# Expert rows of both tables gathered as one, into a ring of 15 places, in a two-block transformer kernel

## The reference

```
qh = (x @ w_q).reshape(tokens, 8 heads, 2, 128);  scores = qh . sub_keys       # 2 x 128 scores a head
s_top, i_top = top_k(scores, 16);  cand = s_top[0] + s_top[1]                  # 16 x 16 sums
c_s, c_pos = top_k(cand, 16);  e_idx = number of the expert at c_pos           # 16 of 16384 experts
g = softmax(c_s);  u = expert_u[e_idx];  v = expert_v[e_idx]                   # rows of 1024 floats
a = gelu(x . u);   out = sum over 8 heads and 16 experts of (g * a) * v
```

## Time and profile before

| | |
|---|---|
| median of 3 runs | 2082.24 us (2077.01 to 2084.2) |
| profiled execution | span 2089.8 us from first to last instruction; its time outside the span is not recorded |
| busy, of the span | TensorE 1440.7, VectorE 1273.9, ScalarE 670.7, GpSimd 716.9 us |
| moved by DMA | 466.82 MB, of which 271.61 MB in the queue that holds the gathers |

### The profile page before, as it was taken

One profiled execution on the slowest core, in us unless ns is written; L12 is line 12 of the kernel. 1 busy time (PEld: TensorE's weight loads), 2 busy tenths in 40 slices (PEclk: granted clock), 3 DMA queues, 4 the chain that ended last, 5 costly groups with the idle time before them and its releaser, 6 DMA issues.

```text
span 2089.8 us, 23542 instructions
## 1 busy us (share of the span) xinstructions
PE 1440.7 (69%) x8468; PEld 1178.3 (56%) x8468; DVE 1273.9 (61%) x2141; ACT 670.7 (32%) x963; POOL 716.9 (34%) x629
## 2 busy tenths in 40 slices
PE   3999999998999999998999824443333233322345
PEld 3889989997889989997889822221111011101111
DVE  2655665554645665555445787676767676777763
ACT  2544635444544544444554411101111101111101
POOL 1010000000110000004000177677777777776775
PEclk8999999999999999999999967777677666767679
DMA  9644454655543455654545489898988888888897
GB/s 169 203 141 135 141 182 152 192 187 158 181 142 122 150 173 162 195 189 138 168 138 162 139 295 330 302 313 307 319 309 318 282 301 294 310 311 303 309 354 259
DMA packets 236976, 466.82 MB, mean 223 GB/s; under 512 B 15960, under 2 KB 136968, under 8 KB 236856
## 3 DMA queue, kind: packets, MB, share of 16 engines
q0 software_dynamic: 74432, 271.61, 37.7%
q1 hardware_dynamic: 162424, 193.65, 28.9%
HBM read 461.02 MB, written 4.19 MB: 223 GB/s over the span
## 4 chain that ended last, share of the span: by engine, by line
PE 45%; issue 14%; DMA 13%; DVE 12%; POOL 11%; ACT 4%; SPq 0%; DVEq 0%; POOLq 0%; ACTq 0%
POOL arena L1994 11%; PE acc L537 9%; PE acc L539 9%; PE acc L538 9%; DMA arena<-in_peer_v,arena 9%; PE att L537 3%; DMA arena<-in_w_in 3%; PE att L539 3%; PE att L538 3%; DVE w_lo L532 2%; ACT w_hi L526 2%; PE acc L1495 2%; PE acc L1496 1%; DVE arena L1846 1%; PE att L640 1%
## 5 line engine op out<-in xcount | busy, mean ns | idle before, releaser
L532 DVE TENSOR_TENSOR w_lo<-arena,w_hi 128x2048 fp32r<-128x2048 f32 x176 | 404.6, 2300 | 330.6 <-ACT w_hi L526 327.9
L1495 PE MATMUL acc<-arena,gate_raw 128*128 128x512 f32 x256 | 166.1, 735 | 543.6 <-DMA arena<-in_peer_v,arena 515.2
L1495 PEld LDWEIGHTS acc<-arena,gate_raw 128*128 128x128 f32 x256 | 46.2, 218 | 650.0 <-DMA arena<-in_peer_v,arena 570.6
L526 ACT CAST w_hi<-arena 128x2048 fp32r<-128x2048 f32 x176 | 334.8, 1905 | 211.8 <-DMA arena<-in_w_in 71.9
L1994 POOL DMA_INDIRECT arena<-in_peer_u,arena x256 | 340.0, 1328 | 167.9 <-issue 73.1
L1846 DVE SCALAR_TENSOR_TENSOR arena<-arena 128x1024 f32<-128x1024 f32 x256 | 302.2, 1221 | 62.1 <-DMA arena<-in_peer_u,arena 60.8
L1994 POOL DMA_INDIRECT arena<-in_peer_v,arena x256 | 304.7, 1190 | 84.5 <-issue 71.7
L1859 DVE SCALAR_TENSOR_TENSOR x_res<-arena,x_res 128x1024 f32<-128x1024 f32 x128 | 164.5, 1285 | 197.4 <-DMA arena<-in_peer_v,arena 195.9
L537 PE MATMUL acc<-xa_hi,w_hi 128*128 128x256 f32 x928 | 269.8, 291 | 20.3 <-DVE w_lo L532 17.6
L538 PE MATMUL acc<-xa_hi,w_lo 128*128 128x256 f32 x928 | 265.1, 286 | 0.0
L539 PE MATMUL acc<-xa_lo,w_hi 128*128 128x256 f32 x928 | 265.0, 286 | 0.0
(11 more groups left out here) (259 smaller groups left out, 2695.5 us busy)
## 6 DMA issues: line engine op xcount, KB each, us to landing
arena<-in_w_in SPq DMA_DIRECT2D x72, 1024.0 KB
arena<-in_w_up SPq DMA_DIRECT2D x32, 1024.0 KB
arena<-in_w_down SPq DMA_DIRECT2D x32, 1024.0 KB
arena<-in_w_branch_m SPq DMA_DIRECT2D x8, 1024.0 KB
arena<-in_w_branch_a SPq DMA_DIRECT2D x8, 1024.0 KB
arena<-in_w_out SPq DMA_DIRECT2D x8, 1024.0 KB
arena<-in_peer_w_q SPq DMA_DIRECT2D x8, 1024.0 KB
arena<-toep SPq DMA_DIRECT2D x2, 2048.0 KB, 11.7
```

The lines of the kernel that those rows point to most:

```text
L526: nc.scalar.copy(w_hi[:, s, :], raw[r]).then_inc(S["hi_ready"], mark("hi_ready", ("u2" if second else "u", u)))
L532: nc.vector.tensor_tensor(w_lo[:, s, :], raw[u % RAW_RING], w_hi[:, s, :].bitcast(F32), ALU.subtract).then_inc(S["lo_ready"], mark("lo_rea ...
L1495: nc.tensor.matmul(sums[0][:], diag[j // 2 % 2], rows_ring[j][:, 0:512], start=first, stop=last)
```

## The change

The two tables are laid side by side outside the timed kernel, so that row e holds the `u` row and then the `v` row of expert e: 8 KB. One gather brings both. There are 256 "items" n (256 gathers of 1.049 MB). `rows_ring` has 15 places of 8 KB a partition. Five (`EARLY`) are free when the attention part is over; the other ten (`LATE`) lie over `xb_hi`, `xb_lo`, the `w_hi` and `w_lo` rings and the `raw` buffers, and are free when the last unit `pq` 7 is done. The first ten items use the five early places only.

VectorE now does only dots (`row_dot`). TensorE does all sums over `v` halves, in groups of four items, with four `diag` buffers; Gelu and the coefficients go by fours too. `route` is cut in four parts, which stand between the dots.

```diff
+GROUP_ROWS = 4
+EARLY, LATE, EARLY_ITEMS = 5, 10, 10
+def ring_places():
+    return [n % EARLY if n < EARLY_ITEMS else (n - EARLY_ITEMS + EARLY) % (EARLY + LATE) for n in range(ITEMS)]
...
-        rows_ring = [area("bias", i * D, D) for i in range(4)] + [area("mo", i * D, D) for i in range(2)]
-        rows_ring += [area("mv", 0, D), area("ak", 1296, D)]
+        rows_ring = [area("bias", 0, ROW), area("bias", ROW, ROW), area("mo", 0, ROW), row_over("xa_hi", 0), row_over("xa_lo", 0)]
+        rows_ring += [row_over("xb_hi", 0), row_over("xb_lo", 0)] + [row_over("w_hi", i) for i in range(RING)]
+        rows_ring += [row_over("w_lo", i) for i in range(RING)] + raw
-        diag = [gate_flat[:, i * P:(i + 1) * P] for i in range(2)]
+        diag = [gate_flat[:, i * P:(i + 1) * P] for i in range(4)]
...
+            def rows_times_coefficients(q):
+                t = q * GROUP_ROWS // SLOTS
...
+                for n in range(q * GROUP_ROWS, (q + 1) * GROUP_ROWS):
+                    first, last = n % SLOTS == 0, n % SLOTS == SLOTS - 1
+                    pe.wait_ge(S["diag_ready"], n + 1)
+                    nc.tensor.matmul(row_sums[t][0][:], diag[n % 4], rows_ring[PLACE[n]][:, D:D + 512], start=first, stop=last)
+                    nc.tensor.matmul(row_sums[t][1][:], diag[n % 4], rows_ring[PLACE[n]][:, D + 512:ROW], start=first,
+                                     stop=last).then_inc(S["rows_multiplied"], 1)
...
-                    odd_rows(i - 2)
+                    if i in (5, 6):
+                        rows_times_coefficients(i - 5)
...
+            def group_diagonals(q):
+                n0 = q * GROUP_ROWS
+                if n0 % P_TOP == 0:
+                    weight_exp(n0 // P_TOP)
+                d = dots[:, n0:n0 + GROUP_ROWS]
+                act.wait_ge(S["rows_used"], n0 + GROUP_ROWS)
+                nc.scalar.activation(d, d, ACT.Gelu).then_inc(S["gelu_ready"], mark("gelu_ready", q))
+                act.wait_ge(S["coef"], at("coef", q))
+                for n in range(n0, n0 + GROUP_ROWS):
+                    if n >= 4:
+                        act.wait_ge(S["rows_multiplied"], n - 4 + 1)
+                    nc.scalar.activation(diag[n % 4], ident[:], ACT.Copy, scale=dots[:, n:n + 1]).then_inc(S["diag_ready"], 1)
...
+            def row_dot(n):
+                row = rows_ring[PLACE[n]][:, 0:D]
+                dve.wait_ge(S[f"gathered{PLACE[n]}"], 16 * (USES_BEFORE[n] + 1))
+                nc.vector.scalar_tensor_tensor(row, row, 1.0, hn[:, n // SLOTS, :], ALU.mult, ALU.mult,
+                                               accum_out=dots[:, n:n + 1]).then_inc(S["rows_used"], 1)
...
-                    experts(i - 1, later)
+                    if later:
+                        split_lo(dve, later, True)
+                    if i == 2:
+                        dve.wait_ge(S["xn_ready"], at("xn_ready", TT - 1))
+                        for part in range(4):
+                            route(1, part)
+                    elif i == 3:
+                        for n in range(0, 4):
+                            row_dot(n)
+                    elif i == 4:
+                        row_dot(4)
+                        coefficients(0)
+                        for n in range(5, 8):
+                            row_dot(n)
+            for part in range(2):
+                route(2, part)
+            for n in range(8, ITEMS):
+                row_dot(n)
+                if n % GROUP_ROWS == 0:
+                    coefficients(n // GROUP_ROWS - 1)
+                g, k = n // P_TOP, n % P_TOP
+                if g + 2 < ALL_HEADS and k % 4 == 2:
+                    route(g + 2, k // 4)
...
+            for n in range(ITEMS):
+                if n % P_TOP == 0:
+                    g = n // P_TOP
+                    pool.wait_ge(S["expert_ready"], at("expert_ready", (g // P_HEADS, g % P_HEADS)))
+                if n == EARLY_ITEMS:
+                    pool.wait_ge(S["unit_done"], at("unit_done", ("u2", len(units2) - 1)))
+                if USER_BEFORE[n] is not None:
+                    pool.wait_ge(S["rows_multiplied"], USER_BEFORE[n] + 1)
+                nc.gpsimd.indirect_dma_start(
+                    rows_ring[PLACE[n]], None, A["peer_uv"], bass.IndirectOffsetOnAxis(ap=expert[:, n:n + 1], axis=0)
+                ).then_inc(S[f"gathered{PLACE[n]}"], 16)
```

More of the change, by code:

```diff
@@ L121 @@
     "best_diff": "scores less the largest", "best_exp": "their exp, with its sum", "wrec": "one over it",
-    "weight": "the softmax", "rows_used": "a row of the ring has been used",
+    "weight": "the softmax", "rows_used": "a row's first half times the tokens is summed",
     "gelu_ready": "the experts' activations", "coef": "times the softmax",
@@ L127 @@
 }
-SIGNALS |= {f"w_loaded{i}": "" for i in range(RAW_RING)} | {f"gathered{i}": "" for i in range(GATHER)}
+SIGNALS |= {f"w_loaded{i}": "" for i in range(RAW_RING)} | {f"gathered{i}": "" for i in range(EARLY + LATE)}
 def bucket_onehot():
@@ L1535, in second_pe @@
                     rank_keys(i - 1)
-                    odd_rows(i - 2)
+                    if i in (5, 6):
+                        rows_times_coefficients(i - 5)
             rank_keys(P_HEADS - 1)
-            for step in range(P_HEADS - 2, ALL_HEADS + 2):
-                odd_rows(step)
+            for q in range(2, ITEMS // GROUP_ROWS):
+                rows_times_coefficients(q)
         def second_act(act):
@@ L1815, in route @@
[L1815 to L1820 removed]
+                    dve.wait_ge(S["picked"], at("picked", (t, h, 1)))
@@ L1835, in u_rows @@
-            def u_rows(g, unit_to_split):
-                t = g // P_HEADS
-                dve.wait_ge(S["xn_ready"], at("xn_ready", t))
-                for r in range(HEAD_ROUNDS):
-                    if r == HEAD_ROUNDS // 2 and unit_to_split is not None:
-                        split_lo(dve, unit_to_split, True)
-                    for j in range(GATHER):
-                        dve.wait_ge(S[f"gathered{j}"], r * 16 + 16 * (u_block(g) * HEAD_ROUNDS + 1))
-                        dot = dots[:, g * P_TOP + r * GATHER + j:g * P_TOP + r * GATHER + j + 1]
-                        nc.vector.scalar_tensor_tensor(rows_ring[j], rows_ring[j], 1.0, hn[:, t, :], ALU.mult, ALU.mult,
-                                                       accum_out=dot).then_inc(S["rows_used"], 1)
@@ L1926, in second_dve @@
                 if (name, i) == ("pq", 0):
-                    experts(0)
+                    for part in range(4):
+                        route(0, part)
                 elif name == "pq" and i >= 2:
-                    experts(i - 1, later)
-            for step in range(P_HEADS - 1, ALL_HEADS + 2):
-                experts(step)
-                if step == P_HEADS + 4:
+                    if later:
+                        split_lo(dve, later, True)
+                    if i == 2:
+                        dve.wait_ge(S["xn_ready"], at("xn_ready", TT - 1))
+                        for part in range(4):
+                            route(1, part)
[16 more added lines that the diff above has]
+                    route(g + 2, k // 4)
+                if n == SLOTS + 10:
+                    v_sum(0)
+                elif n == SLOTS + 32:
                     last_norm_dve(0)
+            coefficients(ITEMS // GROUP_ROWS - 1)
             v_sum(1)
```

261 lines of the change are left out of this document (106 added, 155 removed).

## The result

The changed kernel takes 1913.04 us (median of 4 runs, 1912.62 to 1913.72) against 2083.22 us (4 runs, 2077.01 to 2086.81), a ratio of 0.918 (95% interval 0.9159 to 0.92). The profiled execution took 1912.72 us with a span of 1911.0 us, where the forecast's sum had 1977.

A forecast was written before the change was run, and what follows sets the result against it. The prediction took DMA plus a hole a head, which eight places can't bridge, as the bound. Its sum 1257 + 3 + 697 + 20 = 1977 us of span, 112.5 less, gave 1970 us, range 1925 to 2020.

The forecast's parts named there:

- The rate: DMA for the gathered rows once kept full: 370 GB/s, 2.83 us an item, from 350 at a share of 0.95.
- hole: Once a head, four microseconds at 123 GB/s while GpSimd idles 4.51 us; the deeper ring removes it, the main gain.
- GpSimd stops being close to a bound: Gather issues: 512 become 256, needing 320 to 590 us, far below 256 x 2.8 us of data.
- a line through two queues' packet times: DMA packets: 6 ns fixed and 0.0447 ns a byte, so an 8 KB row would save 2%.
- Rival 1: DMA wires have a lower ceiling, 350 GB/s or 3.0 us an item: 2010 us in the metric; chance 0.2.
- Rival 5: Gathers of 8 KB rows run at 400 GB/s, 2.62 us an item: metric 1917 us; chance 0.1.
- Rival 2: GpSimd pays for two descriptors a row and is the bound at 3.2 us an item: 2060 us; chance 0.05.
- Rival 3: TensorE at half clock becomes the bound at 3.42 us an item: 2117 us in the metric, slower; chance 0.05.
- Rival 4: Ring doesn't bridge, places held over 30 us after landing: DMA share stays 0.87, 3.42 us an item; chance 0.03.
- The start: Before the late places open: first gather into a late place at 1257 us, ends 1240 and 1275.
- The tail: From the last landing to the end: 1.2 dot, 1.3 to first product, 6.9 for four items, 11.0 after: 20.4 us.
- The metric: Span to median time: 112.5 us of span gain taken from 2082.2, giving 1970 us.

The follow-up runs named there:

- e1: Changed kernel with each item as two gathers of 4 KB from separate tables into the same 15 places; 1981.09 us, ratio to before 0.9498.
- e2: As e1, but VectorE's dot takes only 512 of the 1024 columns; 1929.45 us, a single run.
- e4: Changed kernel with SyncE loading items 10 to 255 as two plain 4 KB loads each, choice of rows left out; 1931.2 us, a single run.
- e3: Changed kernel with SyncE loading items 10 to 255 as plain loads of 8 KB rows, choice of rows left out; 1913.58 us, a single run.
- e7: Changed kernel with a ring of 11 places in place of 15; 1910.46 us (2 runs), ratio to before 0.9143.
- e8: Changed kernel with the routing of a head in one piece, not in four parts; 1913.88 us (4 runs), ratio to before 0.919.
- e11: Changed kernel with VectorE taking the odd items' second sums and TensorE the even ones; 1907.9 us (4 runs), ratio to before 0.9134.

## Why the prediction was right or wrong

**The rate is the step that failed.** It stands in "What would the wires give if kept full? The eleven stretches have 350 GB/s at a share of 0.95, so 367 at a share of 1.00". The stretches weren't limited by wires. The four that are shown have 23 issues each, and with 0.30 us behind each GpSimd's list was occupied for 26.48 + 6.9 = 33.4 of 35 us, 25.09 + 6.9 = 32.0 of 36, 25.43 + 6.9 = 32.3 of 36 and 27.24 + 6.9 = 34.1 of 34. The 4 us that the best one has left are the start of the next hole: its last issue ends at 1515.6, and the next line of GpSimd is

```profile
1520.07 1.68 POOL L1994 DMA_INDIRECT arena<-in_peer_u,arena  x1 [4.50 <-DVE arena L1846]
```

That was to be seen before the run; I read a busy time of 567 of 770 us as an engine with room. Over the whole stretch of the kernel before, GpSimd's groups are:

```profile
L1994 POOL DMA_INDIRECT arena<-in_peer_u,arena x226 | 300.2, 1328 | 136.1 <-DVE arena L1846 67.5 <-issue 64.5 <-PE acc L1496 3.5
L1994 POOL DMA_INDIRECT arena<-in_peer_v,arena x224 | 265.8, 1186 | 74.0 <-issue 62.4 <-PE acc L1496 11.2 <-DVE x_res L1859 0.3
```

566 us busy and 127 us of gaps: 693 of 770. Only 82 us, 11%, are waits for VectorE and TensorE, the "hole". The kernel before was bound by GpSimd's issues plus a hole, and not by DMA plus a hole. That is read from its trace; no run changes the issues of the kernel before alone. e1 shows the issues as the bound directly in the new structure, and e2 and e4 show that 4 KB rows could have had 409. The change in the gathers' number, which the prediction booked at no more than "GpSimd stops being close to a bound", was worth some 50 of the 170 us, and the row size 17, both with 15 places.

The rest, about 102 us between the kernel before and e1 (107 by the profiled spans), can be read from GpSimd's list. From the first issue to the last, the kernel before has 645 us of issues, 154 of gaps (512 x 0.30) and 78 of waits; e1 has 562, 154 and 45. So quicker issues are the larger part (83 us; a mean of 1.26 us before, 1.10 in e1), and fewer waits the smaller (33 us); some 9 us go the other way at the two ends. "So the hole goes away: this is the main gain" had the order wrong. That the issues are quicker because VectorE lost its additions fits e2, but wasn't tested by itself, and neither was the ring with the additions left in place.

**A share near 1 was no ceiling.** 0.99 goes with 374 GB/s in e1, 1.03 with 409 in e2 and e4, 1.01 with 421. The time of a packet isn't a constant either: at the same sizes, 0.377 x 16 x 2089.8 / 74432 = 169 ns before, 0.366 x 16 x 1927.7 / 74432 = 152 ns in e2. So a line through two queues' packet times could not give the speed of full wires. From e3 and e4, at full supply, 4096 bytes take 16 x 4096 / 409 = 160 ns and 8192 take 16 x 8192 / 421 = 311: 9 ns fixed and 0.037 ns a byte. The fixed part was nearly right (6), the slope (0.0447) was a fifth too high.

**Rival 1**, the lower ceiling, is refuted by 421 GB/s. The Trainium skill gives 358 GB/s for one core in "DMA: Bandwidth & Descriptors", Specifications, and the prediction priced that. The same page of the Trainium skill, under "Measured (HBM→SBUF, 128 partitions, SWDGE, issued from GpSimd)", has 425 GB/s for 16 MB with the other core of the pair idle; an estimate by that figure is 2.47 us an item. The trace agrees with the second figure (421 to 422 GB/s, 2.49 us), which the prediction left out. The Trainium skill's "dramatic" gain ("Perfetto Trace Analysis", DMA Optimizations) is for batching from 2 KB to 4 or 8 KB: from 4 to 8 KB the runs give 3%, and none has rows of 2 KB.

**Rival 5** came nearest in its number (1917 us), but its reason, faster bytes in 8 KB rows, holds for only 3%.

**Rival 2** is refuted: 37568 packets. **Rival 3**: TensorE keeps up. Its granted clock is 0.93 in the window above where the mean was 0.71, the four items of the last group took 1.79 us each where half clock would be 3.4, and it still waits for ScalarE's diagonals between groups. The rival's own sum was off by 4: 1257 + 3 + 841 + 20 is 2121, not 2125. **Rival 4**: the ring bridges, by e7 and e8 with four places or a cut routing to spare, each taken alone; the 15 us a place were 13.9.

**VectorE** is no bound, as said, and e11 shows that it would be none with half the sums.

**The start** was mis-sized by 11.6 us. The prediction had rows and weights "here by 1213". The weights of unit 6 landed behind 5 MB of gathers and ScalarE waited for them until 1221; the dots 5 to 7, booked by 1231, and the last split behind them came later. Group 0 itself began at 1228.5 and not 1220, since its Gelu stands behind that wait on ScalarE's list; unit 7 then followed group 1, which ended at 1262.5 and not 1250.

```profile
1221.48 1.90 ACT L529 CAST w_hi<-arena 128x2048 fp32r<-128x2048 f32 x1 [13.96 <-DMA arena<-in_peer_w_q]
```

```profile
1237.88 1.23 DVE L1849 SCALAR_TENSOR_TENSOR arena<-arena 128x1024 f32<-128x1024 f32 x1 [10.00 <-DMA arena<-in_peer_uv,arena]
...
1246.43 2.28 DVE L535 TENSOR_TENSOR w_lo<-arena,w_hi 128x2048 fp32r<-128x2048 f32 x1
```

Group 0 freed places from 1232, the forecast had items 5 to 7 issued from 1222. That "each microsecond of it counts in full" is what the account above shows.

**The tail** was 17.9 us against 20.4. The four items took 7.15 us (6.9 forecast), and from TensorE's last product to the end it was 8.5 us, not 11.0.

**The metric.** I subtracted the gain in span from the median. But the profiled execution before was longer than its kernel's median: its span alone was 7.6 us above it. The one after has a time 1.7 us above its span and lies on its median. So 1977 of span would have been 1979 in the metric, not 1970. This slip took 9 us off a forecast that was too high, which is luck.

## What to carry to other kernels

Before an engine that issues transfers is called idle, add the gap behind each issue to its busy time: count times (duration + gap). A stretch with a high DMA share isn't a measure of what the wires can give; what it can give shows when nothing waits to be issued, and a kernel with plain loads in place of the gathers measures that in one run. Once DMA runs full to the end, the time is the gate's time plus items times pace, so look for the edits that open the gate earlier, and find the ring's depth by runs: trip over pace is its lower bound (7.8 places here, where 8 lost 6% and 11 lost nothing).

## What the runs showed of the hardware

- One gather's issue of 128 rows costs 0.93 us on GpSimd at the least, for rows of 4 KB and of 8 KB (changed kernel) alike, plus 0.30 us. Beside VectorE's two-input passes single issues take up to 1.97 us (e1's timeline above); with the passes halved the mean fell from 1.09 to 0.95 us (e2).
- DMA from the tables reached 421 to 422 GB/s with 8 KB rows (changed kernel, e3) and 409 with 4 KB (e2, e4), gathered or loaded plainly.
- The busy share of the DMA engines doesn't tell how much more they can move: 0.99 at 374 GB/s in e1, 1.03 at 409 in e2.
- In the changed kernel the wires are nearly done some 7 us before the last dot may start. The windows 1880 to 1890 and 1890 to 1900 us have 227 and 7 GB/s, and the dot starts at 1893.15. Why the landing is told so late stays open; with a pause in the stream (e8) 138 GB/s still flowed between 1890 and 1900, and its last dot started at 1896.87.
